# Last norms of two recurrences interleaved with the attention set-up, and heads alternated in the recurrences' small matmuls

## Chip, cores and metric

One core of one Trainium2 chip runs the whole program in one launch. The metric is the device time in microseconds (us) of that core. All data are float32. Each float32 matmul of the program shows in the trace as two MATMUL records with two weight loads; a transpose shows as one.

## What is computed

The reference is one inference step of a 2-layer decoder trunk on 592 tokens: a prompt of 16 + 512 = 528 tokens and 8 sampled sequences of 8 tokens each. Each layer is a mixer with three groups of heads side by side (latent attention, gated linear attention "GLA", and an mLSTM), an output projection with a layer norm, and a top-2 mixture of 16 experts. What matters here is the mixer:

```python
(cq, ckv, kr, gq, gk, gv, ga, gr, mu, mv, mi, mf, mo) = jnp.split(h @ w_in, ...)
q = (rms_norm(cq, mla_q_norm) @ mla_w_uq).reshape(B, T, MLA_HEADS, MLA_NOPE + MLA_ROPE)
q_nope, q_rope = q[..., :MLA_NOPE], rope(q[..., MLA_NOPE:], pos)
c_kv, k_rope = rms_norm(ckv, mla_kv_norm), rope(kr, pos)
q_lat = jnp.einsum('bthn,rhn->bthr', q_nope, w_ukv[..., :MLA_NOPE])
o_lat = mla_prompt_attend(...) or mla_sample_attend(...)      # past is a paged cache of 2048 rows
o_mla = jnp.einsum('bthr,rhv->bthv', o_lat, w_ukv[..., MLA_NOPE:])
S_new, o = run_chunks(gla_chunk, S0, gla_in, lead, chunk)     # state carried over chunks
o_gla = rms_norm(o, gla_norm) * silu(gr)
(Cs, ns, ms), hc = run_chunks(mlstm_chunk, st0, ..., lead, chunk)
hc = hc * sigmoid(mo)
o_ml = head_norm(hc) * ml_norm + ml_skip * uc
y = jnp.concatenate([o_mla, o_gla, o_ml], -1) @ w_out
```

## The kernel before, in words

Activations lie transposed: 128 features in the partitions, 592 tokens along. An instruction stream is written out for each of five engines (PE, DVE, ACT, POOL, and SP, which issues most loads); they meet in counting semaphores and, between stages, in a barrier (`barrier`, L418 in its wait), at which each engine waits for the other four. Every engine works its own stream strictly in the order in which it is written.

PSUM is used as a ring of 8 banks. `group(key, consumer)` takes the next bank for PE; a bank is free again when its consumer ("A" for ACT, "D" for DVE) has read the group that held it eight groups earlier. `drained(key)` makes PE wait until the consumer has read a given group.

One layer runs so:

- **Input projection.** 15 chunks of 128 output features. `project(j, h)` (L510) is one half (296 tokens) of chunk `j`: 8 matmuls, 16 records. The weights go through four slots (`wslot`), which SP fills ahead. Chunks 0 to 7 come first. The 14 halves of the other seven chunks (gr, mo, cq, ckv) are filler work inside the recurrences, dealt out by `late_halves(c)`.
- **Recurrences.** `for c in range(NCH + 1)`: eight prompt chunks of 66 tokens (c = 0 to 7), then the sample chunk (c = 8) with all 64 sampled tokens. In each, PE turns the chunk (`gtok`, `vtok`, `ktok`), makes the scores, runs a late half, makes the GLA output `go` (L605, and L611 with the carried state), the GLA state `gs` (L624), perhaps a second late half, the mLSTM's numerator and denominator `nd` (L640, and L646 with the carried state), and the mLSTM state `mu` (L668). Heads are taken one after the other; heads 0 and 2 write PSUM partitions 0 to 63, heads 1 and 3 partitions 64 to 127. In the sample chunk the carried state is a different one for each sequence, so L611 becomes eight matmuls of 8 columns per head (L608) and L646 eight of 8 columns per head and half (L643). There DVE masks values by sequence (L1657, L1672) before PE can make the states (L618, L656 and L662).
- **Last norms.** ACT squares, PE sums over features with matrices of ones (`gn`, `mm_`, `cqn`, `ckn`, `mvv`), ACT takes Ln and then Exp(-0.5 x) as the inverse root, DVE scales: the GLA and mLSTM outputs into `mix` (L1713 to L1727), the latents `cq` and `ckv` in place (L1720, L1721). Then a barrier.
- **Attention set-up.** PE turns `wukv`, makes the queries (`queries(m)`, L713, 512 prompt tokens; `last_queries(x)`, L720, the other 80), the keys (`kn`, L733), token-major latents (`ctok`), absorbed queries (`qlat`, L747), values (`vtok`, L751). DVE rotates queries and keys (L1734 to L1767), POOL spreads the rotated key over the heads (L2128). Then 17 steps of prompt attention (first scores L762, first maximum on DVE L1776), then four pairs of sampled sequences, whose cache pages POOL gathers (L2141, L2144). Then a barrier.
- **Output projection.** `out_half(m, h)` (L943) with the weights of output chunks 0 to 3 already in the four slots and those of 4 to 7 loaded after the barrier (`wout`). Then norm, router, experts.

Of the kernel before, what the change touches and what calls it, by code (L numbers as in the profile page):

```python
# [20 lines left out]
P = 128  # L21
# [124 lines left out]
def build(nc, I, O, at, ncols):  # L146
    with ExitStack() as ctx:
# [80 lines left out]
        gv, mo = rec.get(2, T), rec.get(2, T)  # L228
        mup = rec.get(2, TP + CONV - 1)
        mus = rec.get(2, NSEQ, TS + CONV - 1)  # L230
        qm = rec.get(GH, T)
        kt, geb = mix[:, 6, :], mix[:, 7, :]
        uc = rec.get(2, T)
        weights_at = rec.n
# [3 lines left out]
        mqw = rec.get(2, 2, T)  # L238
        mk = rec.get(2, T)
        wpb = rec.get(2, T)  # L240
        nd = rec.get(2, 2, T)
        tmp1, tmp2, gb = nd[:, 0, 0, :], nd[:, 0, 1, :], nd[:, 1, 0, :]
        wqk = rec.get(2, 2, P)
# [23 lines left out]
        att = Area(base.n)  # L267
        wukT = att.get(4, P)
        qlat = att.get(NTQ, H)
        ctok = att.get(9, LAT + ROPE)  # L270
        kro = att.get(T)
        mx = att.get(8)
        nmx = att.get(2)
        sums = att.get(8)
        rs = att.get(2)
        kh = att.get(H, Q0)

        assert att.n <= weights_at
        att = Area(weights_at)
        wuq = att.get(2, 1024)  # L280
        wukv = att.get(1024)
        assert att.n <= weights_at + 4 * T + 2 * T

        cq_sq, ckv_sq, ckv_root = mqm[:, 1, :, :], wpb[:, 0, :], wpb[:, 1, :]
        qrR = att.get(NS, H)
        vtok_at = att.n
        vtok = att.get(NPQ, H * MV)
        att.get(PAST + 16 + P - NPQ * H * MV)
        pbuf0 = att.n
        qnt = att.get(4, NTQ)  # L290
        qra = att.get(2, T)
        qrb = att.get(2, T)
        att2 = Area(pbuf0)
        NPB = 3
        pq = att2.get(NPB, 2, QT + Q0)
        pT = att2.get(NPB, 2, Q0 + P)
# [4 lines left out]
        assert att.n <= pbuf0 + NPB * 2 * (QT + Q0)  # L301
        att3 = Area(pbuf0)
        kT = att3.get(2, PAST)
        krT = att3.get(2, 512)
        assert att3.n <= att2.n
        att3 = Area(vtok_at)
        psm = att3.get(PAST + 16)
        osm = att3.get(P)
        assert att3.n <= pbuf0
# [21 lines left out]
        wout = xg_at.get(KD - NSLOT, KD, P)  # L331
# [93 lines left out]
        wlast = {}  # L425

        def wseq(l, what, j):
            return l * (len(CHUNKS) + NSLOT) + (j if what == "in" else len(CHUNKS) + j)
# [5 lines left out]
        def _(pe):  # L434
# [67 lines left out]
            for l in range(DEPTH):  # L502

                barrier(pe, "pe")
                def project(j, h):
                    u = wseq(l, "in", j)
                    wait(f"wslot{u % NSLOT}", 16 * (u // NSLOT + 1))
                    b = group(("in", l, j, h), "DA"[h] if CHUNKS[j][0] != "mu" else "A")
                    for k in range(KD):
                        i = mm(b[:, 0:HALF], wslot[:, u % NSLOT, k, :], xT[:, k, SH[h]], start=(k == 0), stop=(k == KD - 1))  # L510
                    done(i)
                    wlast[u] = ("in", l, j, 1)
# [51 lines left out]
                wait("states_ready", l + 1)  # L564
                for c in range(NCH + 1):
# [29 lines left out]
                    project(*late[0][1:])  # L595
# [6 lines left out]
                    for hd in range(GH):  # L602
                        r = slice(64 * (hd % 2), 64 * (hd % 2) + 64)
                        o = b[r, (hd // 2) * n:(hd // 2) * n + n]
                        mm(o, gtok[0:n, hd * GV:(hd + 1) * GV], am[0:n, hd * n:(hd + 1) * n], start=True, stop=False)  # L605
                        if smp:
                            for s in range(NSEQ):
                                i = mm(o[:, s * TS:(s + 1) * TS], sgs[:, s, :], qm[:, hd, TP + s * TS:TP + (s + 1) * TS],  # L608
# [1790 lines left out]
```

## Time and profile before

| what | value |
|---|---|
| median of 3 runs | 1742.96 us (1740.89 to 1758.02) |
| the profiled execution's own time | 1750.55 us |
| its span from first to last instruction | 1748.8 us |
| TensorE busy / VectorE busy / ScalarE busy | 1435.4 / 696.9 / 433.9 us |
| mean granted TensorE clock | 0.890 of 2.4 GHz |

The span is what the trace covers; 1.75 us of the execution's own time lie around it. The profiled execution was 7.6 us above the median of the timed runs. "Granted clock" is the share of full TensorE speed that the throttle allowed; its two levels are 1.0 (2.4 GHz) and 0.5 (1.2 GHz), and a value between is a mixture over the stretch.

### The profile page before, as it was taken

How to read it: one execution, taken by the hardware profiler on the slowest of the kernel's cores; microseconds unless marked ns; L12 is line 12 of the kernel's file. 1: busy time of each engine (PE TensorE's matmuls, PEld its weight loads, DVE VectorE, ACT ScalarE, POOL GpSimd, SP SyncE). 2: the span in 40 equal slices, each digit the busy share in tenths (PEclk: the TensorE clock that was granted, in tenths of full speed). 3: DMA queues.
4: the chain of work that ended last, by engine and by line, in shares of the span. 5: the costliest groups of instructions: out<-in, count | busy, mean ns of one | idle time of the engine just before them, and what ended most of it. 6: DMA issues, size and time to landing. Idle time of an engine off the chain costs nothing.

```text
span 1748.8 us, 19440 instructions
## 1 busy us (share of the span) xinstructions
PE 1435.4 (82%) x7575; PEld 939.8 (54%) x7575; DVE 696.9 (40%) x1381; ACT 433.9 (25%) x945; POOL 123.8 (7%) x157
## 2 busy tenths in 40 slices
PE   2999997799899579999099999869889966999950
PEld 2767765466667444444077676546666753444420
DVE  3542463556422532222544246345652153223217
ACT  2221211355302312222133111035441140212110
POOL 1000001200100010000210000120010001000002
PEclk9989985899999779999599899579999986999985
DMA  8320102101360149997532010130134104999935
GB/s 273 72 49 25 37 25 55 63 10 61 121 191 2 52 133 346 324 349 233 172 67 61 25 37 25 30 88 10 61 121 149 69 4 161 321 302 350 300 109 165
DMA packets 190988, 220.73 MB, mean 126 GB/s; under 512 B 47992, under 2 KB 164168, under 8 KB 188712
## 3 DMA queue, kind: packets, MB, share of 16 engines
q1 hardware_dynamic: 173800, 152.25, 28.8%
q0 software_dynamic: 12336, 49.82, 8.1%
q10 hardware_dynamic: 4752, 17.30, 2.5%
q8 instruction: 65, 1.06, 0.3%
q14 instruction: 35, 0.29, 0.1%
HBM read 187.48 MB, written 31.83 MB: 125 GB/s over the span
## 4 chain that ended last, share of the span: by engine, by line
PE 64%; DMA 13%; DVE 9%; issue 6%; ACT 3%; SPq 2%; DVEq 1%; POOL 1%; ACTq 1%; POOLq 0%; PEldq 0%
PE ps L510 14%; DMA over<-in_moe_w_up 9%; PE ps L1014 8%; PE ps L943 7%; PE ps L465 6%; PE ps L1030 3%; SPq L2193 2%; PE ps L713 2%; PE ps L780 2%; PE ps L643 2%; DMA y_rows<-over 1%; PE ps L898 1%; PE ps L822 1%; DVE zT L2058 1%; PE ps L640 1%
## 5 line engine op out<-in xcount | busy, mean ns | idle before, releaser
L1095 ACT ACTIVATE over<-ps 128x512 f32<-128x512 f32 (+11 forms) x390 | 186.4, 508 | 520.2 <-PE ps L510 157.7
L1014 PE MATMUL ps<-over 128*128 128x512 f32 x512 | 235.5, 614 | 26.6 <-DMA over<-in_moe_w_up 24.8
L510 PE MATMUL ps<-xT,wslot 128*128 128x296 f32 x960 | 256.6, 427 | 0.0
L510 PEld LDWEIGHTS ps<-xT,wslot 128*128 128x128 f32 x960 | 186.6, 197 | 58.7 <-issue 7.0
L465 PE MATMUL ps<-const,over 128*128 128x128 f32 (+4 forms) x992 | 152.1, 287 | 74.0 <-DVEq L418 20.1
L465 PEld LDWEIGHTS ps<-const,over 128*128 128x128 f32 (+4 forms) x992 | 117.6, 143 | 124.5 <-issue 46.7
L1014 PEld LDWEIGHTS ps<-over 128*128 128x128 f32 x512 | 97.8, 196 | 143.9 <-issue 115.0
L2018 DVE TENSOR_SCALAR over<-over 128x256 f32<-128x256 f32 x33 | 9.7, 294 | 292.3 <-ACT over L1384 267.5
L1441 DVE COPY over<-ps 128x512 f32<-128x512 f32 (+5 forms) x134 | 68.7, 521 | 124.7 <-PE ps L510 67.6
L1030 PE MATMUL ps<-over 128*128 128x512 f32 x256 | 115.3, 593 | 1.2 <-DVE over L1441 1.2
L1384 ACT ACTIVATE over<-ps 128x256 f32<-128x256 f32 x32 | 12.3, 384 | 253.4 <-PE ps L1014 253.4
L465 PE MATMUL ps<-const,zT 128*128 128x128 f32 x192 | 29.0, 303 | 53.7 <-ACTq L1135 48.1
L1030 PEld LDWEIGHTS ps<-over 128*128 128x128 f32 x256 | 46.3, 190 | 48.5 <-issue 48.5
L2158 POOL DMA_INDIRECT over<-x_rows,fetch x32 | 30.3, 946 | 591.9 <-DVEq L1437 309.4
L943 PE MATMUL ps<-mix,wslot 128*128 128x296 f32 x256 | 65.2, 413 | 1.6 <-PEq L418 1.6
L943 PE MATMUL ps<-mix,over 128*128 128x296 f32 x256 | 66.4, 412 | 0.0
L1446 DVE SCALAR_TENSOR_TENSOR zT<-xT,ps 128x296 f32<-128x296 f32 x32 | 14.8, 462 | 118.4 <-PE ps L943 118.4
L2020 DVE RECIPROCAL over<-over 128x256 f32<-128x256 f32 x33 | 57.8, 1753 | 2.4
L943 PEld LDWEIGHTS ps<-mix,wslot 128*128 128x128 f32 x256 | 48.5, 190 | 17.0 <-PEq L418 2.2
L943 PEld LDWEIGHTS ps<-mix,over 128*128 128x128 f32 x256 | 48.7, 190 | 15.1
L465 PEld LDWEIGHTS ps<-const,zT 128*128 128x128 f32 x192 | 24.0, 159 | 56.9 <-issue 43.1
L780 PE MATMUL ps<-over,zT 96*128 96x512 f32 (+3 forms) x128 | 47.9, 456 | 0.0
(381 smaller groups left out, 1919.9 us busy)
## 6 DMA issues: line engine op xcount, KB each, us to landing
over<-in_moe_w_gate SPq DMA_DIRECT2D x33, 1024.0 KB, 9.8
over<-in_moe_w_up SPq DMA_DIRECT2D x33, 1024.0 KB, 12.2
over<-in_moe_w_down SPq DMA_DIRECT2D x33, 1024.0 KB, 6.4
y_rows<-over ACTq DMA_DIRECT2D x33, 512.0 KB, 7.3
wslot<-in_w_in SPq DMA_DIRECT2D x30, 512.0 KB, 4.0
y_rows<-over SPq DMA_DIRECT2D x1, 4608.0 KB, 13.5
wslot<-in_w_out SPq DMA_DIRECT2D x8, 512.0 KB, 3.7
over<-in_w_out SPq DMA_DIRECT2D x8, 512.0 KB, 6.6
```

The costliest lines, as they stand in the source:

```text
L465: return nc.tensor.transpose(out, in_, ident[0:n, 0:n])
L510: i = mm(b[:, 0:HALF], wslot[:, u % NSLOT, k, :], xT[:, k, SH[h]], start=(k == 0), stop=(k == KD - 1))
L643: i = mm(o[:, s * TS:(s + 1) * TS], cns[:, j, s, x * DH:(x + 1) * DH], mqw[:, j, hd % 2, TP + s * TS:TP + (s + 1) * TS], start=False, stop ...
L713: i = mm(b, wuq[:, k, m * P:(m + 1) * P], cq[:, k, 0:Q0], start=(k == 0), stop=(k == 1))
L780: mm(b[:, o], qh[0:HD, 2 * j + a, i_ * P:(i_ + 1) * P], kh[0:HD, 2 * j + a, 0:(i_ + 1) * P], start=True, stop=False)
L943: i = mm(b[:, 0:HALF], w[:, k, :], mix[:, k, SH[h]], start=(k == 0), stop=(k == KD - 1))
L1014: i = mm(b, xgT[:, e % 2, k, :], wgu[:, e % 2, k, :], start=(k == 0), stop=(k == KD - 1))
L1030: i = mm(b, hT[:, e % 2, f, :], wdn[:, e % 2, f, x * 512:(x + 1) * 512], start=(f == 0), stop=(f == 1))
L1095: rel(f_(dst, src, ACT.Copy), key, "A")
L1441: rel(v.tensor_copy(dst, src), key, "D")
L2020: v.reciprocal(e_h, e_h)
L2193: return sp.dma_start(dst, src, allow_slow_non_contiguous=True).then_inc(S(name), 16)
```

## The change

1. **Heads alternate.** In `go` and `nd` the loops over heads are turned: the two heads of a pair, which write different halves of the PSUM partitions, take turns matmul by matmul, in the prompt chunks and among the 8-column matmuls of the sample chunk. The number of matmuls is the same.
2. **Late halves.** The 14 halves are dealt over the eight prompt chunks (two each in c = 0 to 5, one each in 6 and 7); the sample chunk has none. Before it was two each in 0 to 4, one each in 5 to 8.
3. **Latents in the sample chunk.** ACT squares `cq` and `ckv` at the end of c = 7; PE sums them between `gs` and `nd` of the sample chunk; ACT makes the roots right after; DVE scales the latents and rotates the key (`latents()`) inside the loop over mLSTM heads, behind the second mask.
4. **Set-up woven into the end of the recurrences.** PE turns `wukv` and makes queries 6 and 7 between the state matmuls of heads 0, 1 and those of heads 2, 3; then `last_queries(1)`, queries 4 and 5, the GLA sums `gn`, the mLSTM means `mm_`, `last_queries(0)`, `kn`, queries 0 to 3, the tail transposes, the mLSTM variances `mvv`, `ctok`, `qlat`, `vtok`. ACT and DVE follow in a matching order. The scaling of the GLA and mLSTM outputs into `mix` now stands on DVE between the last rotated query and the copy `qrR`. POOL spreads the key before it sends the normaliser rows out. The barrier is gone on all five engines.
5. **Memory and loads.** The attention's weights `wuq`, `wukv` go into weight slots 0, 1 and 3 as soon as the projections have left them, so the slots hold only three chunks of `w_out` ahead (0 to 2) and five are loaded after the barrier instead of four. Buffers of the attention lie elsewhere; `pq` and `pT` are a little smaller.

```diff
@@ late_halves
-            two = n - (NCH + 1)
+            two = n - NCH
-            return [(x, EARLY + (first + x) // 2, (first + x) % 2) for x in range(2 if c < two else 1)]
+            return [(x, EARLY + (first + x) // 2, (first + x) % 2) for x in range(2 if c < two else 1 if c < NCH else 0)]
@@ PE, go (nd is turned in the same way)
-                    for hd in range(GH):
-                        r = slice(64 * (hd % 2), 64 * (hd % 2) + 64)
-                        o = b[r, (hd // 2) * n:(hd // 2) * n + n]
-                        mm(o, gtok[...], am[...], start=True, stop=False)
+                    for j in range(2):
+                        o = [b[64 * a:64 * a + 64, j * n:(j + 1) * n] for a in range(2)]
+                        for a in range(2):
+                            hd = 2 * j + a
+                            mm(o[a], gtok[...], am[...], start=True, stop=False)
                         if smp:
                             for s in range(NSEQ):
-                                i = mm(o[:, s * TS:(s + 1) * TS], sgs[:, s, :], ...)
+                                for a in range(2):
+                                    i = mm(o[a][:, s * TS:(s + 1) * TS], sgs[:, s, :], ...)
@@ PE, sample chunk, between gs and nd
+                    if smp:
+                        wait("latents_squared", l + 1)
+                        for h in range(2):
+                            b = group(("cqn", l, h), "A")
...
+                        for h in range(2):
+                            b = group(("ckn", l, h), "A")
+                            done(mm(b[:, 0:HALF], ones, ckv_sq[:, SH[h]], start=True, stop=True))
@@ PE, sample chunk, behind mu_n of heads 0 and 1
+                            if j == 0:
+                                wait("att_loaded", 16 * 10 * (l + 1))
+                                for t in range(4):
+                                    b = group(("wukT", l, t), "A")
+                                    done(tr(b[:, 0:P], wukv[:, t * P:(t + 1) * P], P))
+                                wait("latents_done", l + 1)
+                                queries(6)
+                                queries(7)
@@ PE, behind the chunks
+                last_queries(1)
+                queries(4)
+                queries(5)
                 ... gn x4, wait("ml_h"), mm_ x4 ...
-                wait("latents_squared", l + 1)
-                ... cqn, ckn ...
+                last_queries(0)
+                for j in range(4): ... kn ...
+                for m in range(4):
+                    queries(m)
                 ... tailN, wait("ml_hsq"), mvv x4 ...
-                barrier(pe, "pe")
-                ... wukT, last_queries(1), queries 4 to 7, last_queries(0), queries 0 to 3, kn ...
@@ ACT
+                    if c == NCH - 1:
+                        act.wait_ge(S("ml_state"), (NCH + 1) * l + c)
+                        act.drain()
+                        f_(cq_sq, cq, ACT.Square)
+                        sig(f_(ckv_sq, ckv, ACT.Square), "latents_squared")
...
                 f_(qm[:, 0:2, :], og, ACT.Square).then_inc(S("gla_sq"), 1)
+                ... copies of wukT; gn logs; copy of qt 0; kn 0, 1 ...
                 act.wait_ge(S("ml_centred"), l + 1)
                 sig(f_(nd[:, 1, :, :], nd[:, 0, :, :], ACT.Square), "ml_hsq")
+                ... kn 2, 3; queries 0, 1; tailN; mvv logs; Exp of gv, then of mk ...
-                barrier(act, "act")
@@ DVE
+                            if hd == 1:
+                                latents()
+                            if hd == 3:
+                                rotated(6)
+                                rotated(7)
...
                 sig("ml_h")
+                ... qt 1; rotated(4); rotated(5) ...
                 ... mm_ x4; sig("ml_centred") ...
-                ... mix of GLA, latents, mix of mLSTM ...
-                barrier(dve, "dve")
                 ... qr0; queries 2, 3; qh; sig("q_rotated") ...
+                ... mix of GLA (waits gla_root), mix of mLSTM (waits ml_root) ...
                 ... qrR; sig("q_spread") ...
@@ SP
-                sp.wait_ge(S("gla_state"), (NCH + 1) * (l + 1))
-                sp.wait_ge(S("ml_state"), (NCH + 1) * (l + 1))
+                sp.wait_ge(filled, index[("in", l, len(CHUNKS) - 2, 1)] + 1)
                 ... wuq, wukv ...
-                barrier(sp, "sp")
+                sp.wait_ge(filled, index[("in", l, len(CHUNKS) - 1, 1)] + 1)
+                load_out(l, 2)
+                sp.wait_ge(filled, index[("q", l, 3)] + 1)
+                load_out(l, 0)
+                load_out(l, 1)
```

## Rows read from the trace of the kernel before

**Rows 1.** The page: busy time by engine, and shares of the chain that ended last.

```profile
PE 1435.4 (82%) x7575; PEld 939.8 (54%) x7575; DVE 696.9 (40%) x1381; ACT 433.9 (25%) x945; POOL 123.8 (7%) x157
...
PE 64%; DMA 13%; DVE 9%; issue 6%; ACT 3%; SPq 2%; DVEq 1%; POOL 1%; ACTq 1%; POOLq 0%; PEldq 0%
```

**Rows 2.** Stretches of layer 0: engines' busy us (instructions), granted clock, DMA.

```profile
126.00:245.00 119.00, 112.58 (x891) 80.27 (x891) 54.46 (x101) 20.56 (x52) 0.00 (x0) 0.93 0.10 28
262.00:279.80 17.80, 17.80 (x147) 16.57 (x146) 2.75 (x4) 0.00 (x0) 1.50 (x2) 0.50 0.07 17
280.00:298.00 18.00, 12.54 (x26) 4.48 (x25) 9.53 (x13) 3.22 (x4) 2.75 (x8) 0.55 0.15 25
298.00:330.00 32.00, 18.20 (x55) 12.46 (x54) 13.99 (x21) 14.02 (x25) 6.54 (x6) 0.68 0.28 54
330.00:360.00 30.00, 30.00 (x98) 15.79 (x96) 13.81 (x20) 13.19 (x28) 3.89 (x4) 0.88 0.30 100
```

**Rows 3.** Chain of waits, layer 0, late halves of c = 4 to 8: start, us, what.

```profile
195.19 3.99 PE ps L510 x16
...
209.61 4.00 PE ps L510 x16
216.73 3.85 DVE mix L1462
222.25 5.11 PE ps L510 x16
233.61 4.00 PE ps L510 x16
...
245.57 5.40 PE ps L510 x16
```

**Rows 4.** Narrow stretches: `go` and `nd` of c = 1.

```profile
155.94:156.37 0.43, 0.43 (x16) 0.43 (x16) 0.42 (x2) 0.00 (x0) 0.00 (x0) 1.00 0.00 0
160.94:162.29 1.35, 1.35 (x35) 1.35 (x36) 0.00 (x0) 0.42 (x1) 0.00 (x0) 1.00 0.03 7
```

**Rows 5.** Chain of waits, small matmuls of c = 1 and of the sample chunk.

```profile
156.58 0.25 PE ps L624 x8
...
251.22 1.03 PE ps L608 x16
...
256.81 1.90 PE ps L618 x4
...
262.58 1.80 PE ps L643 x16
...
281.73 1.73 PE ps L662 x4
```

**Rows 6.** Chain of waits, matmuls that alternate halves in the sample attention.

```profile
476.01 3.71 PE ps L898 x64
```

**Rows 7.** Groups of instructions between 280 and 359 us: busy, mean ns, idle before.

```profile
L713 PE MATMUL ps<-over 128*128 128x512 f32 x32 | 16.0, 660 | 0.0
...
L1764 DVE TENSOR_TENSOR zT<-over 32x1024 f32<-32x1024 f32 x4 | 4.9, 1217 | 0.1
```

**Rows 8.** Timeline, layer 0, last norms and first steps of the attention.

```profile
312.78 1.28 ACT L1263 ACT_TABLE_LOAD   x1
...
315.30 1.39 DVE L1716 TENSOR_TENSOR mix<-mix,over 128x1184 f32<-128x1184 f32 x1 [13.18 <-ACT over L1263]
...
320.50 1.58 DVE L1727 SCALAR_TENSOR_TENSOR mix<-over,vec,mix 128x592 f32<-128x592 f32 x2
...
322.16 1.11 PE L465 MATMUL ps<-const,over 128*128 128x128 f32 x4 [10.07 <-DVEq L418]
...
361.10 0.69 DVE L1776 TENSOR_REDUCE over<-ps 128x1 f32<-128x512 f32 x1 [8.89 <-PE ps L763]
```

**Rows 9.** Timeline, layer 0, start of the output projection.

```profile
498.80 5.16 SPq L2193 DMA_DIRECT2D over<-in_w_out  x4
...
498.98 6.22 PE L943 MATMUL ps<-mix,wslot 128*128 128x296 f32 x24 [0.80 <-PEq L418]
```

More of the change, by code:

```diff
@@ L564, in _, with queries, last_queries @@
                 wait("states_ready", l + 1)
+                def queries(m):
+                    b = group(("q", l, m), "A" if m < 2 else "D")
+                    for k in range(2):
+                        i = mm(b, wuq[:, k, m * P:(m + 1) * P], cq[:, k, 0:Q0], start=(k == 0), stop=(k == 1))
+                    done(i)
+                def last_queries(x):
+                    b = group(("qt", l, x), "AD"[x])
+                    for m in range(4):
+                        for k in range(2):
+                            i = mm(b[:, m * NTQ:(m + 1) * NTQ], wuq[:, k, (4 * x + m) * P:(4 * x + m + 1) * P], cq[:, k, Q0:T],
+                                   start=(k == 0), stop=(k == 1))
+                    done(i)
                 for c in range(NCH + 1):
@@ L1241, in _ @@
                 f_(qm[:, 0:2, :], og, ACT.Square).then_inc(S("gla_sq"), 1)
-                act.wait_ge(S("ml_state"), (NCH + 1) * (l + 1))
-                f_(cq_sq, cq, ACT.Square)
-                sig(f_(ckv_sq, ckv, ACT.Square), "latents_squared")
-                act.wait_ge(S("ml_centred"), l + 1)
-                sig(f_(nd[:, 1, :, :], nd[:, 0, :, :], ACT.Square), "ml_hsq")
+                for j in range(4):
+                    copy(("wukT", l, j), wukT[:, j, :], bank(("wukT", l, j))[:, 0:P])
                 for j in range(2):
@@ L1250, in _, with two_heads @@
                         log_of(("gn", l, j, h), gv[:, j, SH[h]], 1.0 / GV, cst("epsrms"))
-                for h in range(2):
-                    log_of(("cqn", l, h), lnr[:, SH[h]], 1.0 / 256, cst("epsrms"))
-                for h in range(2):
-                    log_of(("ckn", l, h), ckv_root[:, SH[h]], 1.0 / LAT, cst("epsrms"))
+                copy(("qt", l, 0), qnt, bank(("qt", l, 0))[:, 0:4 * NTQ].rearrange("p (m t) -> p m t", m=4))
+                def two_heads(key, dst, j):
+                    full(act, key)
+                    f_(dst[0:NOPE, 2 * j, :], bank(key)[0:64, :], ACT.Copy)
+                    rel(f_(dst[0:NOPE, 2 * j + 1, :], bank(key)[64:128, :], ACT.Copy), key, "A")
+                for j in range(2):
+                    two_heads(("kn", l, j), kh, j)
+                act.wait_ge(S("ml_centred"), l + 1)
+                sig(f_(nd[:, 1, :, :], nd[:, 0, :, :], ACT.Square), "ml_hsq")
+                for j in range(2, 4):
+                    two_heads(("kn", l, j), kh, j)
+                for m in range(2):
+                    two_heads(("q", l, m), qh, m)
                 key = ("tailN", l)
```

329 lines of the change are left out of this document (156 added, 173 removed).

## The prediction

> **What bounds the kernel now.** I read the page first: TensorE is busy 82% of the span, and 64% of the chain that ended last is TensorE's [rows 1]. So a saving counts where PE itself, or a wait of PE, goes. Next I cut layer 0 into stretches [rows 2]. In the eight prompt chunks (126 to 245 us) PE works 112.6 of 119.0 us at clock 0.93: only fewer or shorter matmuls help there. In `nd` of the sample chunk (262 to 280) PE is busy all the time, at half clock, with 147 tiny records. From 280 to 360, the last norms and the set-up of the attention, PE works 12.5 + 18.2 + 30.0 = 60.7 of 80 us, at clocks 0.55, 0.68 and 0.88. The other engines are far from full there: DVE 9.5 + 14.0 + 13.8 = 37.3, ACT 30.4 us. This stretch is a relay of short chains: PE sums, ACT takes roots, DVE scales; DVE waits 13.18 us for ACT's root, and PE waits 10.07 us for the barrier, which DVE reaches last [rows 8]. Idle PE time and low clock go together here, so closing the gaps pays twice. Layer 1 has the same stretches; I work out one layer and double it.
>
> **The prompt chunks.** A chunk with two late halves takes 209.61 - 195.19 = 14.42 us. c = 5, with one half that DVE copies, takes 12.64, because DVE's reciprocal of 3.85 us starts only after that copy and PE waits for it. c = 6, whose half ACT copies, takes 11.36, c = 7 takes 11.96, and then the sample chunk runs its half for 5.40 us before `go` begins at 250.97 [rows 3]. After the change c = 5 has two halves (14.42; the second covers the reciprocal, as in c = 4), c = 6 is like the old c = 5 (12.64), c = 7 like the old c = 6 (11.36), and the sample chunk has none: `go` begins at 209.61 + 38.42 = 248.0. That gains 2.9 us. Without its half, the sample chunk's `go` depends on its turned values and masked scores, which precede it by some tenths; I add nothing.
>
> **Alternation in the prompt chunks.** `go` of c = 1 starts 16 records in 0.43 us, 27 ns each; `nd` 35 in 1.35, 39 ns each [rows 4]. The columns are the same 66. 27 ns is less than one stream of 66 columns needs (16 records of 296 columns take 3.99 us, 0.84 ns a column [rows 3], so 66 columns 56 ns): two heads in different PSUM halves already run side by side in `go`, where four records of one head follow each other, and only in part in `nd`, where eight do. Alternated, `nd` should run at `go`'s pace: 32 x 12 ns = 0.4 us. `go` gains nothing. It counts in the seven chunks in which PE is the limit: 2.9 us. Bounds: 0 and 3.5.
>
> **The sample chunk.** An 8-column record takes 1.03/16 = 64 ns at full clock (`go`) and 1.80/16 = 113 ns at half clock (`nd`) [rows 5], though 8 columns stream in 7 ns: the load of its 64-column weights sets the pace. Do loads for different PSUM halves overlap? The nearest rows: L624 goes round four quarters and needs 0.25/8 = 31 ns a record, with half as wide weights [rows 5]; L898 alternates halves with 64-column weights and needs 3.71/64 = 58 ns for 128 columns, which one stream would take 107 ns for [rows 6]; L662 alternates at half clock with 1.73/4 = 433 ns for 512 columns, half of one stream's 853 [rows 5]. So I take a halving: `nd` from 8 x (1.80 + 0.40) = 17.6 to 8.8 us, gain 8.8; `go` from 5.8 to 2.9 us, gain 2.9 (if DVE's masks are then late, down to 0). Bounds for both: nothing, and another 4.4 in `nd` if the clock were full.
>
> The twelve records of `cqn` and `ckn` now stand in this path. They cost 12 x 0.25 = 3.0 us at full clock, 6.0 at half. `go` ends in small matmuls after which the clock was 0.50 up to 280 [rows 2], so I take 6.0. ACT's squares (1.9 us) before them lie in the gap between two chunks in which ACT is 80% idle [rows 2], and the roots and DVE's scaling (together some 10 us) lie beside `nd` and the state matmuls, 12 us; DVE was idle there except 2.75 us [rows 2]. Cover is enough by 2 us only; if it isn't, queries 6 and 7 start late, by that much.
>
> **The set-up.** Before, from the end of `nd` to the first maximum: 361.10 - 279.83 = 81.3 us. The floor after the change is PE's work in it at full clock: 12.54 x 0.55 + 18.20 x 0.68 + 30.0 x 0.88 = 45.7 us [rows 2], less 3.0 for `cqn`, `ckn`, less 1 for scores already inside: 41.6. On top: the first matmuls still run at half clock until dense work has lifted it; from 322 to 330 it stayed at 0.5 under dense work, so I put 4 us of loss for those 8. And waits that stay: PE for DVE's third mask (DVE needs some 4 us after `mu_n`, PE has `wukT` and two queries of 3.4 us at half clock, so none); PE for `ml_h` (DVE's chain of some 6 us against 7 us of last queries, queries and `gn`, so none at full clock) and then for the banks of queries 4 and 5, which DVE frees only after `ml_h`, 1 us; ACT's copies of `ctok` behind both Exps, 1.5 to 2 us. Sum 49. The end is checked from DVE's side: behind the last query in PSUM it copies (1.4), adds (4.9 [rows 7]), scales into `mix` (three pairs of 1.58 and 1.39: 6.1 [rows 8]) and copies `qrR` (1.7): 14 us to the first maximum, and PE has about 13 of tail transposes, `mvv`, `ctok`, `qlat`, `vtok` and first scores. Both meet, so the norms into `mix` are hidden only just. Gain: 81.3 - 49 = 32.3 us. Bounds: 44 (clock full at once, no waits) and 60.
>
> **What else is moved.** The loads of `wuq`, `wukv` (ten issues, 10 us on SP) go from the end of the recurrences to about 220 us, beside chunks with hardly any DMA (28 GB/s [rows 2]): free. POOL: the key's spread before the row outputs; the gather of the first pages follows some 10 us later in the order but is not needed before the end of the prompt attention, 50 us on: free. The fifth `w_out` load: the four issues take 5.16 us from 498.80, so the fifth ends about 505.3, and PE wants chunk 3 after three halves of 4.0 us, at 511 [rows 9]. 5.7 us for a landing of 512 KB: costs 0 to 2, I take 1.
>
> **Sum.** Per layer 2.9 + 2.9 + 2.9 + 8.8 - 6.0 + 32.3 - 1.0 = 42.8 us; two layers 85.6. Against the profiled execution that is 1750.6 - 85.6 = 1665; that execution was 7.6 above the median, so the forecast for the median is 1743 - 86 = 1657, rounded to 1658.
>
> **Rivals.**
> - *The loads do not overlap.* Alternation then gives nothing: 2.9 + 2.9 + 8.8 = 14.6 a layer less, 1657 + 29 = 1687. For it: no row shows 8-column matmuls alternating with 64-column weights. Against: rows 6. 8%. The Trainium skill, "TensorE: Matmul & The Clock Gate", Part 3 on packing small matmuls, says just this: a weight load overlaps a running matmul only when the row group differs, and here only the column group does. By that rule this case would be the right one; L624, L662 and L898 speak against it.
> - *The relay stays.* PE runs through its new order at low clock, or DVE and ACT, whose streams are now fuller (DVE about 31 us of work between `nd` and the first maximum), set the end. The set-up then takes 60 us instead of 49: 1657 + 22 = 1679. For it: both engines alternate between norms and evacuation, strictly in order, so each slip moves on. Against: neither is half busy. 20%.
> - *Slower.* Each change of PSUM half makes TensorE finish what runs. Records change halves every two: (16 + 32)/2 = 24 switches in each of 8 prompt chunks and (72 + 144)/2 = 108 in the sample chunk, 300 a layer. Without alternation's gain 28.2 us a layer are left, so it decides from 0.094 us a switch; at 0.2 us (about what a record outlasts the start of the next) 60 us are lost against 28: 1743 + 2 x 32 = 1807. L898's pace, 58 ns with such a switch every two records [rows 6], is against it. 2%.
> - *No visible effect* would need the whole set-up gain to go again; between 498 and the end nothing waits on when the attention ended. 2%.
>
> **Chances.** The forecast's case 68%, with its own range 1638 to 1672 (clock full in `nd` and `cqn`: 7 a layer less; a set-up of 44 to 56). The rest as above. The range takes in both rivals on the near side: 1638 to 1690. Faster by over 1% 0.95, within 1% 0.03, slower 0.02. 1% is about what a measurement of this kernel can tell from no change; the three runs before lie within 1%.
>
> **What would show it.** In the profile after: `nd` of the sample chunk 8 to 9 us long at half clock; `nd` of a prompt chunk about 0.9 to 1.0 us; no barrier at its old place, and from the end of `nd` to L1776's successor 45 to 53 us; the clock at 1.0 within 10 us after `nd`; a wait of about 1 us before `out_half` of chunk 3. Wrong it would be if PE waited over 5 us at one of its waits on ACT or DVE in the set-up (first of all `ml_h`, `ctok`'s bank, the first maximum), or if the clock stayed at 0.5 through the queries.

## The result and the profile after

The changed kernel takes 1655.34 us (median of 4 runs, 1650.09 to 1668.25), the kernel before 1750.49 in the four runs beside it (1740.89 to 1760.44). The ratio is 0.9487, 95% interval 0.9446 to 0.9528. The profiled execution took 1656.69 us with a span of 1654.9 us, against 1748.8 before: 93.9 us less, at a mean granted clock of 0.915 instead of 0.890.

The page of the kernel after, busy times and shares of the chain that ended last:

```profile
PE 1379.6 (83%) x7575; PEld 892.5 (54%) x7575; DVE 698.6 (42%) x1381; ACT 440.1 (27%) x949; POOL 126.9 (8%) x157
...
PE 64%; DMA 14%; DVE 8%; issue 6%; ACT 3%; SPq 2%; DVEq 1%; ACTq 1%; POOL 1%; POOLq 0%; PEldq 0%
```

PE executes the same 7575 matmul records as in [rows 1], but is busy for 55.8 us less. Nothing was taken out of its work: its records are shorter, because the clock is higher and because the small ones overlap. The other 38 us of the 93.9 are idle PE time that went.

To see where, I cut both traces at the same instructions. Each stage is the time from one line's first or last record to the next line's (us, worked out from single records of the two traces):

| stage | before, layers 0 / 1 | after | gain |
|---|---|---|---|
| first projection to first 8-column `go` | 211.3 / 207.8 | 203.7 / 200.3 | 7.6 / 7.5 |
| `go`, `gs`, and now `cqn`, `ckn` | 11.4 / 11.4 | 15.1 / 14.1 | -3.8 / -2.7 |
| 8-column part of `nd` | 17.1 / 17.1 | 6.6 / 4.8 | 10.5 / 12.3 |
| end of `nd` to first maximum | 81.5 / 81.4 | 49.8 / 48.6 | 31.7 / 32.8 |
| first maximum to output projection | 137.9 / 137.6 | 137.9 / 138.4 | 0 / -0.8 |
| output projection to first expert | 128.2 / 128.6 | 127.2 / 127.6 | 0.9 / 1.0 |
| experts, to the next layer or the end | 252.6 / 285.2 | 260.1 / 280.6 | -7.5 / 4.5 |

Up to the first maximum the layers gain 46.1 and 49.8 us. The experts' stage, which the change doesn't touch, differs by several us between any two executions (251.7 to 260.1 in layer 0 over all traces of this study); here it takes 3 us of the gain back.

The same stretches of layer 0 as in [rows 2], after: from where to where, engines' busy us (instructions) in the order PE, PE weight load, DVE, ACT, POOL, then granted clock, DMA share, GB/s.

```profile
126.00:245.00 119.00, 113.41 (x944) 80.08 (x943) 56.86 (x108) 22.68 (x55) 0.00 (x0) 0.94 0.15 32
...
258.60:265.60 7.00, 7.00 (x146) 6.54 (x146) 3.52 (x6) 3.11 (x5) 0.00 (x0) 0.68 0.01 2
265.60:285.00 19.40, 19.40 (x69) 9.83 (x68) 15.36 (x24) 5.79 (x11) 4.72 (x9) 0.85 0.09 21
285.00:300.00 15.00, 15.00 (x55) 8.29 (x53) 7.52 (x12) 10.64 (x20) 3.73 (x4) 1.00 0.14 35
300.00:313.00 13.00, 11.49 (x42) 6.47 (x42) 11.75 (x15) 8.99 (x18) 5.31 (x6) 0.74 0.77 243
```

The 146 records that filled 17.8 us at clock 0.50 now fill 7.0 us. From the end of `nd` to 300 us PE is never idle, and in the second row of that stretch the clock is 1.00. Of the old relay one wait is left. The waits of PE from 265 to 314 us (line that waited, for whom: total us, times, longest):

```profile
PE ps L480 <- ACT over L1112: 1.5, 1, 1.5
```

That is a transpose waiting for ACT, which takes both inverse roots (`Exp`, L1300 and L1301) before it copies the token-major latents (L1112). The chain of waits over `nd` and the set-up (start, us, what):

```profile
253.09 4.24 PE ps L665 x8
257.33 1.27 PE ps L669 x4
258.60 0.26 PE ps L681 x4
258.86 1.03 PE ps L685 x32
259.89 0.26 PE ps L681 x4
260.15 1.04 PE ps L685 x32
261.19 0.41 PE ps L681 x4
261.60 1.81 PE ps L685 x32
...
278.14 3.48 PE ps L581 x8
281.62 2.00 PE ps L730 x8
283.62 2.00 PE ps L735 x8
...
290.84 6.87 PE ps L581 x16
...
298.53 1.94 ACT over L1107 x4
...
300.54 1.28 ACT L1300
...
304.75 2.15 PE ps L766 x16
306.90 6.36 PE ps L770 x8
313.26 0.86 PE ps L781 x2
```

Three things are to be read here. First, L685 is the 8-column matmul of `nd`, once L643 [rows 5]. 32 records take 1.81 us at half clock and 1.03 at full, which is what 16 records took before (1.80 for `nd` at half clock, 1.03 for `go` at full): 57 ns instead of 113, 32 instead of 64. The halving is exact at either clock. Second, in `nd` the clock came up and fell again: its first two rounds run in full, the later ones at half, although the engine runs without a gap. What stands before it has changed: the dense sums `cqn` and `ckn` (L665, L669; 12 records of 296 columns) where `gs` stood before. The last four sum records run at half clock for part of their time (1.27 us instead of 1.0), and the small ones after them at full. Third, the relay is gone from the chain: queries, sums and keys (L581, L730, L735, L739) follow each other on PE, and ACT has only some 6 us, from 298 on.

The timeline at the first maximum, and the chain at the output projection:

```profile
315.21 0.69 DVE L1803 TENSOR_REDUCE over<-ps 128x1 f32<-128x512 f32 x1 [3.02 <-PE ps L782]
```

```profile
453.12 12.20 PE ps L960 x48
465.31 0.50 PE ps L484 x2
465.81 3.99 PE ps L960 x16
```

DVE waits 3.02 us for PE's scores, not PE for DVE: DVE's norms into `mix` were done in time. And chunk 3 of the output projection (the second L960 row) starts without a gap: the fifth load that the change moved behind the barrier costs nothing.

### The profile page after: what moved, and what is told of

The parts are those of the page before. It is cut to its first block, busy times and chain, and to the rows that moved or that the text cites. A ratio compares the mean times of both kernels' runs of the same rounds, so it can differ in the third digit from the quotient of the medians.

```text
span 1654.9 us, 19434 instructions
## 1 busy us (share of the span) xinstructions
PE 1379.6 (83%) x7575; PEld 892.5 (54%) x7575; DVE 698.6 (42%) x1381; ACT 440.1 (27%) x949; POOL 126.9 (8%) x157
## 4 chain that ended last, share of the span: by engine, by line
PE 64%; DMA 14%; DVE 8%; issue 6%; ACT 3%; SPq 2%; DVEq 1%; ACTq 1%; POOL 1%; POOLq 0%; PEldq 0%
PE ps L524 15%; DMA over<-in_moe_w_up 10%; PE ps L1031 8%; PE ps L960 8%; PE ps L480 6%; PE ps L1047 3%; SPq L2220 2%; PE ps L799 2%; PE ps L581 2%; DMA y_rows<-over 1%; PE ps L917 1%; PE ps L841 1%; DVE zT L2085 1%; PE ps L494 1%; PE ps L484 1%
## 5 line engine op out<-in xcount | busy, mean ns | idle before, releaser
L1112 ACT ACTIVATE over<-ps 128x512 f32<-128x512 f32 (+11 forms) x390 | 186.5, 508 | 433.5 <-PE ps L524 151.7
L524 PE MATMUL ps<-xT,wslot 128*128 128x296 f32 x960 | 252.9, 422 | 0.0
L480 PE MATMUL ps<-const,over 128*128 128x128 f32 (+4 forms) x984 | 149.6, 284 | 54.1 <-DVEq L1457 10.5
L960 PE MATMUL ps<-mix,over 128*128 128x296 f32 x320 | 83.1, 413 | 0.0
L1404 ACT ACTIVATE over<-ps 128x256 f32<-128x256 f32 x32 | 12.3, 385 | 256.8 <-PE ps L1031 256.8
L960 PEld LDWEIGHTS ps<-mix,over 128*128 128x128 f32 x320 | 60.7, 190 | 19.2 <-DMA over<-in_w_out 0.4
L960 PE MATMUL ps<-mix,wslot 128*128 128x296 f32 x192 | 48.6, 413 | 1.6 <-PEq L428 1.6
L1326 ACT ACTIVATE over<-ps,over 128x512 f32<-128x512 f32 (+3 forms) x68 | 35.2, 524 | 46.0 <-DVEq L1457 17.9
## 6 DMA issues: line engine op xcount, KB each, us to landing
over<-in_moe_w_up SPq DMA_DIRECT2D x33, 1024.0 KB, 12.2
```

Source lines behind the costliest of these rows:

```text
L480: return nc.tensor.transpose(out, in_, ident[0:n, 0:n])
L524: i = mm(b[:, 0:HALF], wslot[:, j % NSLOT, k, :], xT[:, k, SH[h]], start=(k == 0), stop=(k == KD - 1))
L960: i = mm(b[:, 0:HALF], w[:, k, :], mix[:, k, SH[h]], start=(k == 0), stop=(k == KD - 1))
L1112: rel(f_(dst, src, ACT.Copy), key, "A")
L1326: i = f_(d, bank(key)[:, o], ACT.Exp, bias=nmq[:, n % NPB, m:m + 1], scale=SCALE, accum_out=smq[:, n % NPB, a:a + 1])
```

## The experiments

All edits are against the changed kernel unless said otherwise. None leaves work out. Ratios are to the kernel before, run beside each. Stage lengths are from each kernel's own trace, cut as in the table above. Apart from the experts' stage they repeat from trace to trace within about 1 us, or within 3 where the clock may differ; medians of the changed kernel alone came out at 1655.34 and 1659.89, so differences of under some 6 us are read from stages and not from medians.

**Heads in turn again, and alternation alone.** The first keeps everything but the order of heads in `go` and `nd`; the second puts that order, and nothing else, into the kernel before.

```diff
@@ PE, nd (go alike)
-                    for j in range(2):
-                        for x in range(2):
-                            o = [b[64 * a:64 * a + 64, ...] for a in range(2)]
...
+                    for hd in range(MH):
+                        r = slice(64 * (hd % 2), 64 * (hd % 2) + 64)
+                        for x in range(2):
...
```

> The changed kernel with only the alternation undone: in go and nd the heads stand one after the other again. Theory (loads for different PSUM halves overlap): a prompt chunk with two late halves goes from 13.97 back to 14.42 us; nd of the sample chunk from 6.6 and 4.8 us to about 13 to 17.6, go from 3.8 to 5.8; in all 12 to 15 us a layer, so 24 to 30 us more than the changed kernel, 1680 to 1685, ratio to before 0.960 to 0.965. Rival (loads do not overlap, the shorter nd comes from a raised clock alone): nd stays at 5 to 9 us, the kernel within 5 us of the changed one.

> The kernel before with only the alternation added. Theory: nd of the sample chunk 17.1 to 8.5 us at half clock, go 5.8 to about 3 (with the masks of DVE then late by up to 1 us), 0.45 us in each of seven chunks: 12 to 14 us a layer, 1722 to 1726, ratio 0.983 to 0.986. If alternation and the new order help each other through the clock, the two experiments on alternation differ: here nd stays at half clock (8.5 us), in the changed kernel it came to 6.6 and 4.8. Rival: same as before.

Measured: heads in turn 1693.01 us (ratio 0.9682, 0.9642 to 0.9722); alternation alone 1713.98 (0.982, 0.9791 to 0.9848). The chain over the start of `nd`, heads in turn:

```profile
268.30 1.03 PE ps L681 x16
...
274.05 1.80 PE ps L681 x16
```

And alternation alone, its windows over the whole of `nd` (columns as above):

```profile
251.72:260.20 8.48, 8.48 (x144) 8.03 (x142) 2.45 (x4) 0.00 (x0) 1.50 (x2) 0.50 0.15 37
```

The first rows are the clean comparison: at full clock, heads in turn take 1.03 us for 16 records where alternated ones take it for 32. The last row has `nd` in 8.3 us at clock 0.50 (17.1 before, at 0.50): order alone halves it, with no help of the clock. So the rival "the loads do not overlap" falls. The Trainium skill, "TensorE: Matmul & The Clock Gate", Part 3, on packing small matmuls, has a load overlap only where the row group differs; here both heads have the same rows and different columns, and they overlap: 32 records in 1.03 us where 16 in turn take 1.03.

The worth of alternation is larger than expected (24 to 30 us): some 31 us alone (1744.93 to 1713.98) and 27 to 38 inside the change (27 and 34 by the ratios, 33 and 38 by the medians). Each layer shows why. To the start of `go` 2.9 to 6.9 us, the stage from `go` to `nd` 4 to 5, `nd` 8.8 at equal clock (6.5 to 10.4 inside the change, where the clock differs). Of the 6.9, 3.1 us lie ahead of the second late half of layer 0, where the clock differs from one execution to the next: up to the first late half it is 0.94 in alternation alone and in three kernels of other edits, 0.91 in the rest, the kernel before among them. From the second late half on, the two layers gain 3.9 and 2.9.

In the kernel before, alternation also takes 3.4 to 3.8 us from the set-up, which I had not counted (77.7 and 78.0 us instead of 81.5 and 81.4). The windows over `qlat` and `vtok` in layer 0, first of the kernel before, then of alternation alone, place 3.3 us of it:

```profile
350.50:359.20 8.70, 8.70 (x27) 5.38 (x27) 1.67 (x4) 4.36 (x12) 0.00 (x0) 0.61 0.19 44
```

```profile
330.50:335.80 5.30, 5.30 (x26) 3.27 (x26) 1.58 (x4) 4.10 (x11) 0.00 (x0) 1.00 0.31 72
```

The same records run at full clock there, and in layer 1 as well; why the clock holds is open. The attention behind them gives part of it back: 140.9 and 138.7 us instead of 137.9 and 137.6.

**Barrier alone, order alone.** The first puts the barrier back on the five engines behind the last norms, PE behind `mvv`. The second has no barrier, but PE, ACT and DVE do the set-up's work after the norms, as before the change.

```diff
@@ barrier back: PE behind mvv; ACT, DVE, POOL, SP alike
+                barrier(pe, "pe")
@@ norms first: PE (ACT and DVE in the same order)
-                                wait("latents_done", l + 1)
-                                queries(6)
-                                queries(7)
...
-                last_queries(1)
-                queries(4)
-                queries(5)
                 ... gn, mm_, tailN, mvv ...
+                last_queries(1)
+                for m in range(4, 8):
+                    queries(m)
+                last_queries(0)
...
```

> The changed kernel with its new order, and the barrier put back on all five engines behind the last norms (PE behind mvv, ahead of the token-major latents). Theory (the gain of the set-up is the interleaved order; the barrier alone costs what PE then waits for DVE's scaling into mix): PE waits from the end of mvv to the end of DVE's mix, 300 to 310.5 us, and then works its 13 us of ctok, qlat, vtok: first maximum 8 to 11 us later, less the copy qrR that is then hidden, so 7 to 10 us a layer, 1670 to 1675, ratio 0.954 to 0.957. Rival (the barrier was the main cost): the set-up back near 70 us, 1695 or more.

> The changed kernel without a barrier, but with the set-up matmuls, rotations and evacuations behind the last norms, as their order was before. Latents are still normed in the sample chunk and heads alternate. Theory (order counts): PE idles again in the relay of squares, sums, roots (some 10 us a layer), and the clock drops there; end of nd to first maximum 60 to 66 us instead of 49.8 and 48.6: 1680 to 1690, ratio 0.960 to 0.966. Rival (removing the barrier is what counts): within 5 us a layer of the changed kernel, 1655 to 1665.

Measured: barrier back 1679.29 us (0.962, 0.9591 to 0.965), set-up 61.6 and 60.9, so 10 to 12 us a layer more than the changed kernel's in its two traces, where 7 to 10 were expected; norms first 1680.85 (0.9646, 0.96 to 0.9692), set-up 63.0 and 62.2, as expected. Waits of PE in the set-up, barrier back:

```profile
PE ps L480 <- DVEq L428: 10.6, 1, 10.6
```

Norms first, waits and windows (columns as above):

```profile
PE ps L699 <- DVEq L1452: 4.6, 1, 4.6
PE ps L480 <- ACT over L1104: 3.7, 1, 3.7
PE ps L724 <- DVEq L1452: 3.0, 1, 3.0
```

```profile
261.40:280.00 18.60, 11.01 (x31) 4.25 (x28) 13.33 (x19) 1.58 (x2) 2.50 (x7) 0.61 0.01 2
280.00:300.00 20.00, 16.26 (x50) 10.03 (x51) 7.63 (x11) 10.95 (x19) 12.07 (x11) 0.68 0.37 104
300.00:324.00 24.00, 24.00 (x91) 12.46 (x89) 14.27 (x23) 13.02 (x28) 0.00 (x0) 1.00 0.35 107
```

The set-up of 81.5 us (some 78 with the heads alternated, as in both these kernels) splits so: either half of the step brings it to 61 to 63, both bring it to 49. Both kernels also have the latents normed in the sample chunk, whose sums `cqn` and `ckn` took 6.2 us of the old set-up, 4.9 with the heads alternated; no run separates this from the rest. With the barrier the new order loses 10 to 12 us a layer: 10.6 of wait, and a clock of 0.59 from 300 to 325 us after the gap. Without the barrier but in the old order PE is busy 51.3 of 62.6 us and stands still three times for the short steps of the norms, 11.3 us by the windows and by the list of waits. The clock of 0.61 and 0.68 in those stretches costs the rest: in the changed kernel the stretches up to 300 us show 0.85 and 1.00. So the predicted "closing the gaps pays twice" holds, and it is visible in one row each.

**Late halves, and the sums' place.** One kernel deals the late halves as before (the sample chunk has one, the squares stand in c = 8). The other makes `cqn` and `ckn` ahead of the sample chunk's `go`.

```diff
@@ half in sample
-            two = n - NCH
-            return [... range(2 if c < two else 1 if c < NCH else 0)]
+            two = n - (NCH + 1)
+            return [... range(2 if c < two else 1)]
@@ sums before go: PE, sample chunk, from behind gs to here; ACT's roots ahead of its copy of go
+                    if smp:
+                        wait("latents_squared", l + 1)
+                        for h in range(2):
+                            b = group(("cqn", l, h), "A")
...
                     drained(("gtok", l, c))
```

> The changed kernel with the late halves dealt as before: the sample chunk has one again, and ACT squares the latents behind it. Theory (the half in the sample chunk is on PE's path, while in c = 5 it covers DVE's reciprocal): go of the sample chunk begins 2.5 to 4 us later in each layer, the rest unchanged: 1660 to 1663, ratio about 0.952. Rival: the half only fills a wait for DVE's masks (gs needs them), so up to the sums nothing changes and the kernel stays at 1655 to 1657.

> The changed kernel with the sums of squares cqn, ckn ahead of go in the sample chunk instead of between gs and nd. Theory (the dense 296-column sums right before nd lift the clock for it): nd falls back to half clock, 8.3 us as in the run with alternation only, instead of 4.8 to 6.6; go and gs with the sums get 1 to 3 us shorter, since the sums run at full clock and under DVE's masks. Net 0 to +2 us a layer, 1655 to 1659. Rival (the clock in nd has another cause): nd stays at 4.8 to 6.6 and the kernel gains 1 to 3 us a layer, 1649 to 1653.

Measured: half in sample 1661.72 us (0.9507, 0.9452 to 0.9561); sums before `go` 1653.28 (0.9456, 0.9406 to 0.9507). The chain over `nd`, sums before `go`:

```profile
250.73 2.27 PE ps L659 x4
253.00 0.41 PE ps L681 x4
253.41 1.81 PE ps L685 x32
255.22 0.41 PE ps L681 x4
255.63 1.81 PE ps L685 x32
```

Half in sample came out as expected. With the sums moved away, `nd` falls back to 8.3 us in both layers, all of it at half clock; in the changed kernel it takes 4.8 to 6.6. All traces of the study agree: `nd` has a clock of 0.67 to 1.00 in the sixteen layers with alternated heads and the sums in front, and 0.50 in the eight without the sums. That shows the second reading above: the sums, dense and right in front, lift the clock for `nd`. But they pay for that. They run at half clock themselves: `go` to `nd` is 14.1 to 15.1 us with them between and 6.8 and 6.7 without, and the way to `go`, where they now stand, is 3.1 and 2.8 us longer: there the 12 records run at full clock, 0.25 us each (the chain has six in 1.50 and four in 1.00 us). Net, the place of the sums is worth 1 to 4 us a layer in favour of the earlier one, summed over the three stages, where 0 to 2 us against it were expected; the medians don't separate the two. Half in sample likewise loses 2.5 and 4.4 us up to `go` and gets 3.2 and 1.9 back between `go` and `nd`, and its `nd` runs wholly at full clock (4.8 in both layers): the placing of the halves, a step of the change, is worth little by itself. What stands in front sets the clock of `go` too. Its 8-column part, sums before `go` and then the changed kernel:

```profile
246.55:248.95 2.40, 2.40 (x74) 2.29 (x72) 2.02 (x4) 2.32 (x4) 0.00 (x0) 1.00 0.03 7
```

```profile
243.68:247.47 3.79, 3.78 (x71) 3.54 (x68) 2.91 (x7) 0.00 (x0) 0.00 (x0) 0.56 0.03 6
```

It takes 2.40 us at full clock in both layers of the four kernels in which a late half or the sums stand right before it (alternation alone, half in sample, and both with the sums ahead); in eight other traces, the changed kernel's two among them, where neither does, its clock is 0.50 to 0.88.

**Values early.** PE waits 1.5 us for ACT, which has the roots in front. So I gave PE the four value matmuls (`vtok`) before that point, and in a second kernel also put the GLA root and DVE's GLA scaling later.

```diff
@@ PE (ACT's copies of vtok move likewise, to before tailN)
                 for m in range(4):
                     queries(m)
+                for t in range(NPQ):
+                    b = group(("vtok", l, "a", t), "A")
+                    done(mm(b, ckv[:, t * P:(t + 1) * P], wukv[:, 512:1024], start=True, stop=True))
@@ second kernel: ACT, the same line goes behind the copies of qlat; DVE's GLA scaling behind the prompt attention
-                sig(f_(gv, gv, ACT.Exp, scale=-0.5), "gla_root")
```

> The changed kernel with the values vtok (PE and ACT's copies) ahead of the tail transposes and mvv. In the changed kernel PE ends the set-up with a wait of 1.5 us for ACT and then vtok at half clock (6.4 us for 8 records instead of 3.5). Theory (the end of the set-up is PE's order and clock): vtok runs at full clock, end of nd to first maximum 1 to 3 us shorter a layer, 1650 to 1653. Rival (DVE's scaling into mix sets the end, or ACT, which gets 2.4 us of copies ahead of its roots): no gain or up to 2 us more a layer.

> As the run with early values, and the GLA part of the scaling into mix (3.0 us of DVE) moved behind the prompt attention, where DVE waits for gathered pages, its root (1.2 us of ACT) behind the copies of qlat. Theory (with the values early all three engines meet at the end of the set-up, so relieving DVE and ACT counts): end of nd to first maximum 3 to 6 us shorter a layer than the changed kernel's 49.8 and 48.6, 1643 to 1650, ratio 0.940 to 0.945. Rival (PE alone sets the end): as the run with early values.

Measured: 1673.97 us (0.9589, 0.9532 to 0.9645) and 1672.04 (0.9546, 0.9492 to 0.96): 12 to 19 us above the changed kernel's two medians. Both intervals overlap the changed kernel's second one (0.949 to 0.957, below); what settles it is the attention's stage, longer in all four layers. The theory missed in sign, though `vtok` does run at full clock as it said, in 3.6 us. Windows of values early, from before the first scores on, and the same stretch of the changed kernel:

```profile
296.00:308.20 12.20, 9.75 (x47) 6.47 (x45) 10.99 (x13) 10.29 (x23) 7.09 (x8) 0.78 0.56 174
308.20:320.00 11.80, 11.74 (x26) 6.40 (x26) 4.10 (x13) 1.60 (x6) 0.00 (x0) 0.51 0.40 143
```

```profile
313.10:325.00 11.90, 10.65 (x58) 7.25 (x56) 6.96 (x21) 5.32 (x18) 0.00 (x0) 1.00 0.15 48
```

And the chain of values early at the first scores:

```profile
308.26 2.07 PE ps L781 x2
310.34 2.00 PE ps L782 x2
```

A score that takes 0.86 us in the changed kernel (313.26 in its chain) takes 2.07 here: for 11.8 us PE runs at clock 0.51. The four dense value matmuls had stood between the thin stretch of transposes (`tailN`, `ctok`, `qlat`) and the first scores. Moved ahead, they leave that thin stretch, with PE busy 9.75 of 12.2 us, directly before the scores. The attention then takes 142.8 and 141.6 us instead of 137.9 and 138.4. The half clock lasts 5.5 to 7.7 us beyond the first maximum in all four layers of the two kernels, which makes some 3 to 4 us; in the twelve layers of the kernels with the values behind it is over before that maximum. The set-up is no shorter either (51.4 and 50.3): ACT, with the copies of `vtok` now ahead of its roots, keeps PE waiting for 1.7 us before `ctok` and 0.8 more before the scores, which is the rival that the expectation names. The second kernel gets the set-up to 48.8, and pays the same in the attention (142.8 and 143.6). In the trace of values early, set-up and attention lose 8 to 11 us over both layers; that execution was the fastest of its four, 10 us under their median, so a part of the difference between the medians is not in any trace.

**Roots split.** The remaining wait attacked where it arises: ACT takes the mLSTM root, copies `ctok`, and only then takes the GLA root; DVE scales the mLSTM part first. PE's order stays.

```diff
@@ ACT
-                sig(f_(gv, gv, ACT.Exp, scale=-0.5), "gla_root")
                 sig(f_(mk, mk, ACT.Exp, scale=-0.5), "ml_root")
                 ... copies of ctok ...
+                sig(f_(gv, gv, ACT.Exp, scale=-0.5), "gla_root")
@@ DVE
-                ... mix of GLA (waits gla_root) ...
                 ... mix of mLSTM (waits ml_root) ...
+                ... mix of GLA (waits gla_root) ...
```

> The changed kernel with ACT's two last roots parted: the mLSTM's (Exp of mk) stays, the GLA's (Exp of gv, 1.2 us) moves behind the nine copies of ctok, and DVE scales the mLSTM part into mix first, then the GLA part. Theory (in the changed kernel PE waits 1.5 us for the first ctok copy, in which time the clock falls and vtok runs at half speed, 6.4 us): with a wait of only 0.3 us the clock holds and vtok takes 3.5 us: end of nd to first maximum 2 to 4 us shorter a layer; against the changed kernel in the same call 4 to 8 us less, some 1648. Rival (the clock falls all the same, since what precedes is transposes and small matmuls): 1 us or less a layer, not to be told from the changed kernel.

> Both the parted roots and the sums ahead of go. If the two add: the changed kernel less 4 to 8 us for the roots and 0 to 4 for the sums, 1645 to 1650. If only the sums count, 1651 to 1655.

> The changed kernel once more, unaltered, as the measure for the other two in this call: 1650 to 1660, ratio to before 0.945 to 0.953. Its sample nd may come out at 4.8, 6.6 or 8.3 us, as the clock falls in it.

Measured side by side: roots split 1656.88 us (0.95, 0.9477 to 0.9522), roots split with the sums before `go` 1647.57 (0.947, 0.9435 to 0.9505), the changed kernel once more 1659.89 (0.953, 0.949 to 0.957). Roots split, waits of PE and its chain:

```profile
PE ps L480 <- ACT over L1112: 0.4, 1, 0.4
```

```profile
304.83 1.56 PE ps L766 x16
306.39 5.33 PE ps L770 x8
```

The wait falls from 1.5 to 0.4 us, and the eight records of `vtok` behind it from 6.36 to 5.33: a shorter gap, and less time at half clock. The 3.5 us that were expected of them didn't come: the clock still fell, to 0.68 over `vtok` in both layers (0.55 to 0.70 in the changed kernel's two traces). The set-up is 47.4 and 47.3 us, against 51.3 and 50.0 of the changed kernel beside it (49.8 and 48.6 in its first trace). That is 1 to 4 us a layer, seen in both layers and again in the version with both edits (47.1, 47.2); between the medians it doesn't show. Both edits together came out in the range expected and have the lowest median of the study, 12.3 us under the changed kernel's beside it, but the two intervals overlap, so "some us better" is as much as can be said.

## Why the prediction was right

The forecast was 1658 us, and the ratio of 0.9487 puts the measured time at 1653.5 for the median that it started from. For the two profiled executions it was 85.6 us of gain, and 93.9 were measured.

| term, both layers | predicted | measured |
|---|---|---|
| late halves, alternation in prompt chunks (to `go`) | 11.6 | 15.1 |
| `go` halved, less `cqn`, `ckn` | -6.2 | -6.4 |
| `nd` | 17.6 | 22.8 |
| set-up | 64.6 | 64.4 |
| fifth `w_out` load | -2.0 | 0 |
| rest of the program | 0 | -2.0 |
| sum | 85.6 | 93.9 |

- *What bounds the kernel.* Right: both ways of gaining, fewer gaps and shorter records at a higher clock, were found, and the experiments separate them: the barrier's 10.6 us of wait in one, 11.3 us of PE's waits in the other, the rest clock.
- *Prompt chunks and alternation in them.* The period of a chunk with two halves fell from 14.42 to 13.97 us, so 0.45 against the 0.4 expected: 3.2 us a layer. The other 4.4 of 7.6 are the late halves, 2.9 predicted. About half of that excess is in the last chunks: c = 6 and 7 together, from 221.05 to `go` at 243.68, take 22.6 us where my copy of the old c = 5 and c = 6 gave 24.0, less 0.8 for alternation. I took those chunks' waits over whole. Cut only from the second late half on, ahead of which the clock differs between executions, the stage goes from 108.8 us in both layers to 101.6 and 102.8, with alternation alone to 104.9 and 105.9: so alternation is worth 3 to 4 us and the late halves some 3, both near the 2.9 predicted. In heads in turn the same stage is 208.2 and 203.3 us, in half in sample 206.1 and 204.7: two edits that each account for 2.5 to 4.6 us.
- *`nd` of the sample chunk.* The halving was right, down to the nanosecond. The size was off because I held the clock at 0.50, the level that [rows 2] show: the dense sums which the change itself puts in front lifted it for a part of `nd` in layer 0 and all of it in layer 1. "Another 4.4 in `nd` if the clock were full" was the bound, and layer 1 reached 3.5 of it.
- *`cqn` and `ckn` on the path.* Right at 6.0 a layer in size: the chain shows 4.24 + 1.27 = 5.5 us for them, at half clock, in layer 0. That the whole row comes out at 6.4 against 6.2 is partly luck: `go`, put at full clock, takes 3.8 us in its 8-column part in layer 0 (clock 0.56) and 2.6 in layer 1, against 2.40 at full clock, and the 0.5 saved on the sums covers part of that.
- *The set-up.* 49 predicted, 49.8 and 48.6 measured. The details agree less well than the sum. The clock was back at 1.0 somewhat sooner than the 8 us I had put: 0.85 over the 19.4 us from 265.6 means 5.8 us at half, a loss of 2.9 us and not 4. But it fell once more from 300 to 313 (0.74, a loss of 3.4 us), which I had not foreseen. In exchange PE's waits were fewer: none for `ml_h`, none for the banks of queries 4 and 5, 1.5 us for ACT's copies of `ctok`, the one that had been put at 1.5 to 2. And DVE, which "meets" PE at the first maximum, was 3 us ahead of it.
- *Moved loads, POOL.* Nothing waits for `wuq`, `wukv` or the gather; the fifth `w_out` load costs 0, the lower bound.
- *The rivals.* Loads that don't overlap: fell in the experiments on the order of heads. The relay stays (60 us of set-up): this is what the kernel does when either half of the step is missing, 61 to 63 us; with both it doesn't. Slower by drains at each change of PSUM half: 32 records in 1.03 us with a change of half every two of them are 64 ns from one change to the next, which leaves no room for 0.094 us a switch. No visible effect fell with the result.
- *The range.* The sum holds as written; the lower end doesn't follow from its own terms. 7 us a layer for the clock and a set-up of 44 lead from 1657 to 1633, not 1638, and 44 is called the bound without waits where the floor was worked out as 41.6. Nothing rests on either.
- *The signs.* `nd` of the sample chunk "8 to 9 us at half clock" was true for alternation alone and for sums before `go`, not for the changed kernel, and the wait before chunk 3 of the output projection didn't come. The set-up within 45 to 53 us, the full clock within 10 us after `nd` and no wait over 5 us came as forecast. `nd` of a prompt chunk is 1.00 us long for its 35 records (1.35 in [rows 4]), as forecast:

```profile
160.20:161.20 1.00, 1.00 (x35) 1.00 (x36) 0.00 (x0) 0.42 (x1) 0.00 (x0) 1.00 0.00 0
```

What stays open: what drives the several us by which the experts' stage differs between executions, and whether the order "sums before `go`" is truly better; both are below what the medians tell apart.

## What to carry to other kernels

Where short steps of three engines follow each other, look for dense, independent matmuls of the next stage and weave them in, and take out the barrier as well: here either one left 61 to 63 of 81 us (with the heads alternated and the latents' sums already out of the way), both left 49. Let tiny matmuls take turns between two halves of the PSUM partitions; the number of matmuls stays the same, and here it halved their time. Before moving dense matmuls forward, look at what they stand in front of: the values moved to fill a wait of 1.5 us cost 3 to 5 us a layer in the attention, most of it because the first scores then ran at half clock.

## What the runs showed of the hardware

- Two matmuls that share their rows and differ in the PSUM half overlap in full, weight loads included: 8-column records with 64-column weights go at 32 ns instead of 64 at full clock, and at 57 instead of 113 at half clock. In the single records of the changed kernel's `nd` at full clock two weight loads start 6 ns apart and the next two 55 to 58 ns after them; with the heads in turn every load starts 55 to 59 ns after the last.
- The granted clock of a stretch of tiny matmuls depends on what ran before it. The same 8-column part of `nd` took 8.3 us at clock 0.50 behind `gs` (three kernels, both layers), and 4.8 to 6.6 us behind the dense sums (eight traces; 0.67 to 1.00). In the changed kernel's layer 0 it began at full clock and fell to half after 2.6 us of tiny records, while PE was never idle.
- A thin stretch (PE busy 9.75 of 12.2 us, small transposes) ahead of dense scores was followed by 11.8 us at clock 0.51, though PE was busy 11.74 us of them; with four dense matmuls between, the clock was 1.00 in the first 11.9 us of the scores.
